# The opening of a fused flow-matching trunk: three scale tiles through PE, heads one by one

## The reference

```python
mod = silu(c) @ w_mod + b_mod                  # for c and for c_ctx: two vectors of 6 * 1024
sh1, sc1, g1, sh2, sc2, g2 = jnp.split(mod[:, None, :].astype(x.dtype), N_MOD, axis=-1)
h = rmsnorm(x, p['norm1_g']) * (1 + sc1) + sh1
u, q, k, v, z, xbc, dt_raw = split_sizes(h @ p['w_in'], IN_SIZES)
```

## Time and profile before

| | us |
|---|---|
| median of three runs | 1383.5 (1382.97 to 1384.87) |
| the profiled execution: its time | 1383.34 |
| its span in the trace | 1381.6 |
| PE busy | 1313.4 (95%) |
| DVE busy | 1093.5 (79%) |
| ACT busy | 646.8 (47%) |
| POOL busy | 162.6 (12%) |

### The profile page before, as it was taken

How to read it: one execution, slowest core, us unless ns; L and a number is a source line. 1 busy time by engine, 2 the same in 40 slices (tenths; PEclk the granted TensorE clock), 3 DMA queues, 4 the chain that set the end, 5 groups by cost and what they waited for, 6 DMA issues and landing times.

```text
span 1381.6 us, 20127 instructions
## 1 busy us (share of the span) xinstructions
PE 1313.4 (95%) x7564; PEld 1243.7 (90%) x7564; DVE 1093.5 (79%) x2102; ACT 646.8 (47%) x1035; POOL 162.6 (12%) x166
## 2 busy tenths in 40 slices
PE   5899999999999999999989999999999899999996
PEld 4799889999988999999979988898999799999996
DVE  5889988679857999999967998637877699989432
ACT  4643445644556444442355335445445654454331
POOL 0058000000210000000100930000031000000001
PEclk8999999999999999999999999999999999999998
DMA  9456535323343454447734572333224244454431
GB/s 361 142 203 209 195 107 198 139 96 104 111 147 100 160 168 152 153 160 258 258 134 153 206 249 79 107 107 107 84 101 152 89 155 143 147 168 132 140 126 46
DMA packets 58289, 208.95 MB, mean 151 GB/s; under 512 B 6736, under 2 KB 8912, under 8 KB 56784
## 3 DMA queue, kind: packets, MB, share of 16 engines
q1 hardware_dynamic: 55648, 197.53, 42.7%
q0 software_dynamic: 2544, 10.13, 2.2%
HBM read 203.97 MB, written 3.67 MB: 150 GB/s over the span
## 4 chain that ended last, share of the span: by engine, by line
PE 44%; DVE 37%; issue 8%; ACT 8%; DMA 1%; POOL 0%; SPq 0%; DVEq 0%; ACTq 0%; POOLq 0%
PE acc L823 12%; PE acc L825 12%; PE acc L824 12%; DVE wl L1508 8%; DVE cv L1658 6%; DVE junk_front L1583 5%; DVE junk_ffn L1583 5%; ACT wh L1155 1%; DVE gates L1702 1%; DVE cv L1679 1%; PE mix L1075 1%; DVE al L1513 1%; ACT ah L1172 1%; DVE x L1720 1%; PE mix L980 1%
## 5 line engine op out<-in xcount | busy, mean ns | idle before, releaser
L823 PE MATMUL acc<-hh,wh 128*128 128x384 f32 x1528 | 524.1, 343 | 14.3 <-DVE wl L1508 11.6
L825 PE MATMUL acc<-hh,wl 128*128 128x384 f32 x1528 | 511.3, 335 | 0.0
L824 PE MATMUL acc<-hl,wh 128*128 128x384 f32 x1528 | 511.1, 334 | 0.0
L1508 DVE TENSOR_TENSOR wl<-raw,wh 128x1024 fp32r<-128x1024 f32 (+1 forms) x280 | 344.8, 1233 | 126.1 <-ACT wh L1155 124.4
L1155 ACT ACTIVATE wh<-raw 128x1024 fp32r<-128x1024 f32 (+1 forms) x280 | 290.7, 1041 | 111.2 <-PE acc L825 110.2
L823 PEld LDWEIGHTS acc<-hh,wh 128*128 128x128 f32 x1528 | 286.8, 188 | 35.0 <-DVE wl L1508 20.9
L824 PEld LDWEIGHTS acc<-hl,wh 128*128 128x128 f32 x1528 | 287.0, 188 | 2.4
L825 PEld LDWEIGHTS acc<-hh,wl 128*128 128x128 f32 x1528 | 286.8, 188 | 0.0
L1658 DVE SCALAR_TENSOR_TENSOR cv<-acc,prm,cv 128x1 f32<-128x1 f32 (+1 forms) x416 | 153.7, 412 | 11.3 <-ACT cv L1276 4.2
L823 PE MATMUL acc<-ah,wh 128*128 128x384 f32 x352 | 119.1, 338 | 3.1 <-DVE wl L1508 2.7
L824 PE MATMUL acc<-al,wh 128*128 128x384 f32 x352 | 118.3, 336 | 0.0
(11 more groups left out here) (256 smaller groups left out, 1673.1 us busy)
## 6 DMA issues: line engine op xcount, KB each, us to landing
raw<-in_wstream_dram SPq DMA_DIRECT2D x248, 512.0 KB, 3.5
rawm<-in_wstream_dram SPq DMA_DIRECT2D x80, 512.0 KB, 3.8
raw<-in_wstream_dram SPq DMA_DIRECT2D x32, 448.0 KB, 3.3
head<-in_whead_dram SPq DMA_DIRECT2D x8, 1024.0 KB, 14.0
crow<-in_cvec_rows_dram POOLq DMA_DIRECT2D x2, 1024.0 KB, 5.2
out_y_dram<-gates POOLq DMA_DIRECT2D x8, 192.0 KB, 2.7
prm<-in_par_dram POOLq DMA_DIRECT2D x2, 591.5 KB, 4.3
x<-in_xs_dram SPq DMA_DIRECT2D x1, 1024.0 KB, 8.9
```

The source lines that it names most:

```text
L823: mm(out, sh, mhi, start=start, stop=False)
L824: mm(out, sh, mlo, start=False, stop=False)
L825: return mm(out, sl, mhi, start=False, stop=stop)
L1508: tt(wl[:, s, 0:n], raw[:, raw_slot(u), 0:n], wh[:, s, 0:n].bitcast(F32), ALU.subtract).then_inc(lo_done, 1)
```

## The change

It has five parts, all of them in the opening.

1. The scale blocks of heads 2, 4 and 6 (`PE_SCALE`) are no longer summed on DVE. PE transposes them (eight 128x128 transposes into the banks `acc[3]` and `misc`), ACT copies them to `wt` (two of 128x512), and PE then takes their products as it does for a shift, in the second half of `mix6`.
2. Heads are taken one at a time (`head_products`, `head_copy`, `head_sums`, `head_scale`), each with its own small piece of a PSUM bank.
3. `first_joint` replaces the first `joint`: products with h tile j-2 stand around the head products of j.
4. The affine step goes from ACT to DVE (`first_affine`, two tensor_scalar instructions with two column operands); the h tiles use four ring buffers instead of two. The two row tiles `crow` are copied out of PSUM by DVE, not ACT.
5. SP loads x first, then heads 0 and 1, three weight tiles, heads 2 to 7 and the parameters of layer 0. POOL no longer loads these, and no longer clears `cv`. The small cast to `selr` moves behind the first u unit.

```diff
+PE_SCALE = (2, 4, 6)
...
-            load_head(0)
             sp.dma_start(x[:, :, 0:LAT], xs).then_inc(x_in, 16)
             sp.dma_start(x[:, :, CTX0:T], xp).then_inc(x_in, 16)
-            for j in range(1, KT // 2):
-                load_head(j)
+            load_head(0)
+            load_head(1)
             for i, (l, kind, u) in enumerate(STREAM):
                 if i == JOINT:
-                    for j in range(KT // 2, KT):
+                    for j in range(2, KT):
                         load_head(j)
+                    sp.dma_start(prm[:, :], par[0]).then_inc(par_in[0], 16)
...
+            def head_transposes(j):
+                n = PE_SCALE.index(j)
+                pe.wait_ge(head_in[j], 16)
+                if n == 0:
+                    pe.wait_ge(rs_ready, 1)
+                for half in range(2):
+                    if n:
+                        pe.wait_ge(wt_in, 2 * n + half - 1)
+                    for i in range(4):
+                        last = nc.tensor.transpose(wt_bank[half][:, P * i:P * i + P],
+                                                   head[:, 2 * j + 1, P * (4 * half + i):P * (4 * half + i) + P], ident)
+                    last.then_inc(wt_done, 1)
+            def head_products(j):
+                if j:
+                    pe.wait_ge(part_in, j)
+                pe.wait_ge(head_in[j], 16)
                 for k in range(KT):
                     g = k % 4
-                    last = mm(mix6[32 * g:32 * g + 32, 0:2 * P], cpad[:, k, :], head[:, 4 * p:4 * p + 3:2, P * k:P * k + P],
+                    last = mm(mix6[32 * g:32 * g + 32, 0:P], cpad[:, k, :], head[:, 2 * j, P * k:P * k + P],
                               start=(k < 4), stop=(k >= 4))
+                if j in PE_SCALE:
+                    n = PE_SCALE.index(j)
+                    for k in range(KT):
+                        g = k % 4
+                        if g == 0:
+                            pe.wait_ge(wt_in, 2 * n + k // 4 + 1)
+                        last = mm(mix6[32 * g:32 * g + 32, P:2 * P], cpad[:, k, :], wt[:, n, k, :],
+                                  start=(k < 4), stop=(k >= 4))
                 last.then_inc(part_done, 1)
-            def shift_sums(p):
-                pe.wait_ge(part_in, p + 1)
-                if p >= 2:
-                    pe.wait_ge(mod_read, p - 1)
-                for i in range(2):
-                    last = mm(shift_bank[p][:, 2 * i:2 * i + 2], part[:, P * i:P * i + P], tab_("sel")[:, 0:2],
+            def head_sums(j):
+                pe.wait_ge(part_in, j + 1)
+                for i in range(2 if j in PE_SCALE else 1):
+                    last = mm(head_bank[j][:, 2 * i:2 * i + 2], part[:, P * i:P * i + P], tab_("sel")[:, 0:2],
                               start=True, stop=True)
                 last.then_inc(head_done, 1)
+            def first_joint():
...
+                for j in range(2, KT + 1):
+                    if j in PE_SCALE:
+                        head_transposes(j)
+                    if j == 2:
+                        for i in range(JOINT):
+                            wait_lo(pe, i)
+                    pe.wait_ge(h_hi, count(0, NSPLIT, SP_N1 + j - 2))
+                    for i in range(JOINT):
+                        high_products(j - 2, i)
+                    if j < KT:
+                        head_products(j)
+                    pe.wait_ge(h_lo, count(0, NSPLIT, SP_N1 + j - 2))
+                    for i in range(JOINT):
+                        low_product(j - 2, i)
+                    if j < KT:
+                        head_sums(j)
+                pe.wait_ge(h_hi, count(0, NSPLIT, SP_N1 + KT - 1))
+                high_products(KT - 1, 0)
+                pe.wait_ge(h_lo, count(0, NSPLIT, SP_N1 + KT - 1))
+                for i in range(JOINT):
+                    if i:
+                        high_products(KT - 1, i)
+                    low_product(KT - 1, i).then_inc(unit_used, 1)
...
-            shift_pair(0)
             first_squares()
-            shift_sums(0)
-            shift_pair(1)
-            shift_sums(1)
+            for j in range(2):
+                head_products(j)
+                head_sums(j)
+            pe.wait_ge(crow_ready, 2)
+            first_joint()
             for l in range(DEPTH):
                 if l:
...
+            def head_copy(j):
+                if j in PE_SCALE:
+                    n = PE_SCALE.index(j)
+                    for half in range(2):
+                        act.wait_ge(wt_done, 2 * n + half + 1)
+                        af(wt[:, n, 4 * half:4 * half + 4, :].rearrange("p k c -> p (k c)"), wt_bank[half],
+                           ACT.Copy).then_inc(wt_in, 1)
+                act.wait_ge(part_done, j + 1)
+                if j:
+                    act.wait_ge(head_done, j)
+                n = 2 * P if j in PE_SCALE else P
+                af(part[:, 0:n], mix6[:, 0:n], ACT.Copy).then_inc(part_in, 1)
+            def first_high(j):
+                act.wait_ge(affine_done, j + 1)
+                high(0, None, hh[:, j, :], ring[j % 4])
             def first_norm():
-                for j in range(KT):
-                    b = cv[:, j % 2, :]
-                    act.wait_ge(h_full, F_N1 + j + 1)
-                    if j % 2 == 0 and 2 <= j <= KT - 4:
-                        shift_part(j // 2 + 1)
-                    act.wait_ge(scale_ready, j // 2 + 1)
-                    affine(b, sc1, 0, j)
-                    high(0, None, hh[:, j, :], b)
...
-            for v in range(2):
-                act.wait_ge(rows_made, v + 1)
-                af(crow[:, v, :], rows_ps[:, v, :], ACT.Copy, scale=2.0).then_inc(crow_ready, 1)
...
+            def first_full(j):
+                if j >= 4:
+                    dve.wait_ge(h_lo, count(0, NSPLIT, SP_N1 + j - 4))
+                tt(ring[j % 4], x[:, j, :], rs[:, :], ALU.mult).then_inc(h_full, 1)
+            def first_affine(j):
+                dve.wait_ge(h_full, F_N1 + j + 1)
+                b = ring[j % 4]
+                for v, (a0, a1) in enumerate(SEGS):
+                    last = ts(b[:, a0:a1], b[:, a0:a1], sc1[:, j, v:v + 1], mod[:, j, v:v + 1], ALU.mult, ALU.add)
+                last.then_inc(affine_done, 1)
+            def first_low(j):
+                low(0, SP_N1 + j, hl[:, j, :], ring[j % 4], hh[:, j, :])
...
+            def head_scale(j):
+                bank = head_bank[j].rearrange("p (t v) -> p t v", v=2)
+                if j in PE_SCALE:
+                    dve.wait_ge(head_done, j + 1)
+                    step.then(tt(mod[:, j:j + KT + 1:KT, :], bank,
+                                 bm[:, j:j + KT + 1:KT].unsqueeze(2).to_broadcast([P, 2, 2]), ALU.add))
+                else:
+                    summed(0, KT + j, KT + j + 1)
+                    dve.wait_ge(head_done, j + 1)
+                    tt(mod[:, j:j + 1, :], bank[:, 0:1, :], bm[:, j:j + 1].unsqueeze(2).to_broadcast([P, 1, 2]), ALU.add)
+                stt(out=sc1[:, j:j + 1, :], in0=mod[:, KT + j:KT + j + 1, :], scalar=1.0,
+                    in1=norm1_weight(0)[:, j:j + 1].unsqueeze(2).to_broadcast([P, 1, 2]), op0=ALU.add,
+                    op1=ALU.mult).then_inc(scale_ready, 1)
+                dve.wait_ge(scale_ready, j + 1)
...
+                    for v in range(2):
+                        dve.wait_ge(rows_made, v + 1)
+                        ts(crow[:, v, :], rows_ps[:, v, :], 2.0, None, ALU.mult).then_inc(crow_ready, 1)
                     scale_sums(0)
                     scale_sums(1)
-                    scale_pair(0)
-                    first_norm(0)
+                    dve.wait_ge(rs_ready, 1)
+                    for j in range(4):
+                        first_full(j)
+                    for j in range(2):
+                        head_scale(j)
+                        first_affine(j)
                     for u in range(AHEAD):
                         lo(l, u)
-                    scale_pair(1)
-                    first_norm(1)
-                    scale_sums(2)
-                    scale_pair(2)
-                    first_norm(2)
-                    scale_sums(3)
-                    scale_pair(3)
-                    first_norm(3)
-                    for j in (KT - 2, KT - 1):
-                        low(0, SP_N1 + j, hl[:, j, :], cv[:, j % 2, :], hh[:, j, :])
-                    dve.wait_ge(tab_in, 16)
-                    nc.vector.tensor_copy(selr[:, :], tab_("heads")[:, 8:12])
+                    first_low(0)
+                    first_low(1)
+                    for j in range(2, KT):
+                        scale_sums(j)
+                        head_scale(j)
+                        first_affine(j)
+                        if j + 2 < KT:
+                            first_full(j + 2)
+                        first_low(j)
```

100 lines of the change are left out of this document (46 added, 54 removed).

## The result

| | us |
|---|---|
| changed kernel, median of four runs | 1391.62 (1390.58 to 1392.59) |
| kernel before, median of four runs beside it | 1384.18 |
| ratio, with its 95% interval | 1.0054 (1.0037 to 1.0072) |
| the changed kernel's profiled execution: its time | 1390.58 |
| its span in the trace | 1388.8 |

The two profiled executions are 7.24 us apart (1390.58 against 1383.34). DVE is busy for the same 1093.5 us as before: six scale sums of 1.22 went, eight affine steps of 0.67 and two crow copies of 1.23 came.

What follows compares the result with a forecast made beforehand. After the opening PE was taken as the bound, so the change counts by when unit 3 starts: 61.0 against 56.47, +4.5. 1383.5 + 4.5 = 1388.0 us, range 1384.8 to 1391.4, the forecast's own 1386.3 to 1389.8.

Steps and rivals of the forecast that it cites:

- Up to the first weight product: Opening up to the first weight product: it starts at 26.75 instead of 30.38, 3.6 us earlier.
- Head 2: Start of head 2's scale on DVE: at 32.05, 5.3 us after the first weight product, or 29.95 at best.
- The chain: Opening loop, two heads a cycle: links across DVE, ACT and PE sum to 8.95 us, against 9.16 a pair before.
- Transposes: Scale blocks on PE: transposes start 0.14 us apart, eight take 1.25; the skill page's figure would make it 2.2.
- Affine: Affine step, new on DVE, 256 and 128 columns: 0.56 us, or about 0.64 at tensor_tensor's pace.
- DVE's own work is all that counts: Rival for the opening loop: DVE's busy time sets it, ending at 47.4, 4.8 us earlier, so 1378.7; chance 0.06.
- The links are shorter: Rival for the loop: PE warm at the restart, a cycle takes 8.7 us, so 1385.5; chance 0.14.
- x does not come earlier: Rival for the opening loads: landing not by order of issue, rs 2.6 us later, so 1390.6; chance 0.05.
- the sum: Whole kernel: median 1383.5 us plus 4.5 for the later start of unit 3 gives 1388.0.
- from there the same distances as before: Stream from unit 3 on: distances unchanged, with unit 3 itself starting at 61.0 against 56.47.
- PE stays cold: Rival: PE at its lower level in the cycles and at unit 3, +1.9 to +3.7, so 1389.9 to 1391.7; chance 0.15.
- gaps of under one us are not followed by the lower level: Kernel before, at 50.05: short PE gaps kept full pace, while idles of 5.16 and 4.07 us were followed by the lower level.

Runs made afterwards that it cites:

- the repeat: The changed kernel run once more without an edit: 1390.32 us (6 runs), ratio 1.0043 to the kernel before.
- The idle products: Changed kernel plus twelve PE products nobody reads, before the sums of head 1, before the first weight product and after the last low products: 1387.84 us, ratio 1.0019.
- the first experiments: Four edits of the changed kernel: wt copies earlier (1386.43 us), no transposes (1387.51), twelve idle PE products (1387.84), sums of head 3 earlier (1388.49).
- x first alone: Kernel before with only x loaded ahead of head 0 and the squares ahead of the first head products on PE: 1383.46 us, ratio 0.9990.
- the repaired whole: Changed kernel with wt copies ahead of the odd hh tile and sums of heads 3, 5 and 7 moved earlier on DVE: 1383.99 us, ratio 0.9997.

## Why the prediction was partly wrong

The direction and the mechanism held; the size did not, and the median lies 0.2 us outside the range.

- *Up to the first weight product.* Forecast 18.6 for rs, measured 18.14 (its second half ran from 17.62 for 0.52); forecast 26.75 for the product, measured 26.29 at the lower pace, as said. The crow copies took 1.23 each (forecast up to 1.3) and were hidden.
- *Head 2.* Forecast 32.05 with 4.3 us of waiting, measured 32.29 with 5.32 (31.61 with 4.53 in the repeat). That the time fits so well is in part luck: from the first product to this scale it took 6.00 us where 5.3 were forecast, and the product came 0.46 early. The idle products moved it to 29.69, so the lower level has 1.9 to 2.6 us of it.
- *The chain.* Forecast 8.95 a cycle and 2.2 of waiting, measured 8.94 and 2.01, and the same twice in the repeat. Link by link it is the row order shown, and moving the wt copies out of it took away 1.62 a cycle.
- *Transposes.* The Trainium skill, "TensorE: Matmul & The Clock Gate", "Part 4: PE-mode transpose", gives about 275 ns for one (bf16); the trace agrees, with a median of 0.273 in float32. Four took 0.63 from the first start to the last end, and the next four started 0.47 behind them (34.68 and 35.15), so they start about 0.12 apart, a little closer than the forecast's 0.14, and PE was not late by them.
- *Affine.* Two pieces took 0.67, but the next DVE instruction started 0.58 after the first (0.56 forecast).
- *DVE's own work is all that counts*, the rival of 0.06, fell twice: DVE waited as said, and with 7.6 us more work it was not done later.
- *The links are shorter* and *x does not come earlier* fell too: cycles of 8.94, PE cold at the restart, and x ending ACT's wait at 10.14.

The step that failed is the sum, 1383.5 + 4.5. It took the distances at full clock from head 2 on, and "from there the same distances as before" behind unit 3. Three terms of it were mis-sized, mostly by TensorE's lower level, and together they are the 2.7 us between 4.5 and the 7.24 of the two profiles:

1. The cycle of head 6 was taken as 8.95 and took 9.62, with PE at its lower level from 49.1 to 52.5. With what follows, unit 3 was +5.34 late, not +4.5. In the repeat this fall was absent, and unit 3 +4.03: the forecast lies between the two.
2. Unit 3 itself ran partly at the lower level, since PE idled 2.48 us in front of it. The ninth weight tile's low part, 72.63 before, came at 78.41 (+5.78) and in the repeat at 77.29 (+4.66). That is 0.4 and 0.6 us, and is the rival "PE stays cold", which had 0.15 where it should have been part of the forecast. The measured 1391.62 lies in that rival's range (1389.9 to 1391.7), but by luck: terms 1 and 2 are 1.3 us together, not its 1.9 to 3.7.
3. The stream behind that tile was taken as unchanged, and was 1.5 us longer in the profile (7.24 less 5.78) and 0.8 in the repeat. In all thirteen profiles its length goes with the time that PE spent at the lower level in it, whatever the opening was:

| at the lower level, 70 to 1365 us | from the ninth tile's low part to the end |
|---|---|
| 0 | 1306.9 |
| 3.4 (kernel before, three others) | 1308.9; 1308.2, 1308.2, 1308.7 |
| 6.8 (the repeat, one other) | 1309.8; 1309.7 |
| 10.2 (changed kernel) | 1310.4 |
| 13.7 | 1311.2, 1311.7 |
| 17.1 | 1312.5, 1312.6, 1312.8 |

   The falls, near 421 and 1097 in the changed kernel and near 703 and 1095 in its repeat, lie in stretches whose instructions the change does not touch. The kernel before had one, at 698, in its profile, and with 3.4 us that profile is among those with the least; its 31 runs beside the first experiments spread from 1382.6 to 1389.5. Whether the change makes falls there likelier, one profile of each kernel can't tell.

The prediction had a sign of all this before it and passed it over. It argued that gaps of under one us are not followed by the lower level, from the products at 50.05. But in the same trace of the kernel before a fall came from 39.6 to 43.0, behind gaps of 0.55 and 0.82:

```profile
39.38 0.54 PE L919 MATMUL acc<-hh,wh 128*128 128x384 f32 x1 [0.82 <-ACT hh L1172]
39.71 0.52 PE L920 MATMUL acc<-hh,wl 128*128 128x384 f32 x1
```

So a loop at full pace from head 2 on was no safe assumption, with or without longer gaps.

The opening thus costs 4.7 to 5.8 us in these two profiles, and the first measurement of 7.4 was high. A run's mean granted clock tells how high:

| mean granted clock | kernel before, mean of its 31 runs beside the first four experiments | changed kernel, its ten runs |
|---|---|---|
| 0.988 to 0.990 | 1384.5, 1383.7, 1383.4 (19 runs) | 1388.5 (one, at 0.989) |
| 0.987 | 1386.2 (2) | 1390.6, 1388.8 |
| 0.986 | 1385.6 (5) | none |
| 0.985 | 1387.3 (4) | 1390.7; 1390.3 (2) |
| 0.982 to 0.984 | 1389.5 (one) | 1392.6 (2); 1392.0; 1391.2 |

At equal clock the two kernels are 2.5 to 5 us apart. Two of the first four runs of the changed kernel had 0.982, and 16 of the 31 of the kernel before have 0.988 or 0.989. Part of the lower clock belongs to the change, since its opening holds more of it (17.1 us at the lower level before 70 us, 20.5 in the repeat, against 13.7); the rest is scatter. How much of the 7.4 is which, ten runs do not settle.

## What to carry to other kernels

When work is taken off a busy engine, write down the chain that then ties the engines together, in each one's instruction order, and compare a turn of it with the busy time: here 8.95 against 6.75, and the place of two ACT copies alone was worth 1.6 us a cycle. Price a new wait twice: once as the wait, and once as the pace of TensorE behind it. When several edits go together, run the simplest of them alone beside the sum: here x first alone brought unit 3 as far forward as the repaired whole. For a difference under half a per cent, read the mean granted clock of each run beside its time before believing a median of four.

## What the runs showed of the hardware

- The same idle gap of PE did not always give the same clock: after 2.74 us it came back at the lower level (0.52 a product), after 2.75 us at the full one (0.34). Which gap is followed by a fall changed with the execution: the norm near 421 in one profile of the changed kernel, a wait near 703 in the other, the norm near 1095 in both.
- The stream behind the opening took 1306.9 us with no time at the lower level and 1312.5 to 1312.8 with 17.1 us of it: about 0.3 us lost for each us at the lower level.
- Idle products ahead of the later norms made the kernel before faster, and the runs lay closer together: 1379.73 to 1382.73, against 1381.12 to 1385.66 beside them.
- A tensor_scalar with two column operands. By the groups by form of the changed kernel (nanoseconds of the shortest, the median and the longest):

```profile
L1629 DVE TENSOR_SCALAR cv<-cv,sc,mod x8: 341/378/416, 20.6 to 46.7; 128x256 f32<-128x256 f32 x4, 128x128 f32<-128x128 f32 x4
```

  The 128 columns more of the longer form cost 0.075 us, 0.59 ns a column; with one operand it is (421 - 287) / 256 = 0.52; tensor_tensor took 0.29 for 128 columns in this trace and 0.558 for 384, 1.05 ns a column. The Trainium skill, "VectorE: DVE Perf Modes", "The perf-mode tier table (the rule you actually need)", doubles the pace of an fp32 tensor_scalar in SBUF; the rows agree for one such operand (2.0 times that of tensor_tensor) and nearly for two (1.8 times), and the part that does not grow with the columns is about 0.05 us larger.
- DVE copied 128x1024 out of PSUM in 1.23 us, ACT in 1.02.
